# Pooling stage in another order: ACT scales x's columns, the values' products stand behind the pooling products, and the router works on x unscaled

## What is computed

```python
def pool_mixer(h, w, b, scale):          # 4 groups of 256 columns, windows 2, 4, 8, 16
    hg = h.reshape(B, S, N_POOL_GROUPS, POOL_GROUP)
    pooled = stack([centred_mean(hg[:, :, g], POOL_WINDOWS[g]) for g in range(4)])
    y = einsum('bsgc,gcd->bsgd', pooled - hg, w) + b
    return y.reshape(B, S, D_MODEL) * scale

def modulated_sublayer(x, mod, g_pre, g_post, fn, weight):
    shift, scale, gate = mod             # rows of silu(c) @ ada_w + ada_b
    h = rmsnorm(x, g_pre) * (1.0 + scale) + shift
    y = rmsnorm(fn(h), g_post)
    return x + weight * (1.0 + gate) * y

kv = rmsnorm_2(mem, g_mem) @ w_mem_kv    # K and V of the memory tokens, used much later

h2 = rmsnorm_2(x, g_ffn)                 # the router and the experts
g_logits = h2 @ w_rg + b_rg              # 4 groups, the best one is taken
e_logits = h2 @ w_re + b_re              # 32 experts, the best 2 of the group
moe = sum(combine[:, n] * swiglu_n(h2) for n in 32 experts)
```

## Time and profile before

| | |
|---|---|
| median of three | 1756.24 us |
| the profiled execution | 1757.07 us, of which the span 1755.0 |
| PE busy | 1660.3 us (95%) |
| DVE, ACT busy | 1216.7 us (69%), 868.3 us (49%) |
| mean granted clock of PE | 0.967 |
| from K's first product to the first product of the second feed-forward | 239.2 to 319.4 us |
| x behind the mixing to the first expert | 1406.8 to 1438.6 us |

### The profile page before, as it was taken

One profiled execution on the slowest core, in us unless ns is written; L12 is line 12 of the kernel. 1 busy time (PEld: TensorE's weight loads), 2 busy tenths in 40 slices (PEclk: granted clock), 3 DMA queues, 4 the chain that ended last, 5 costly groups with the idle time before them and its releaser, 6 DMA issues.

```text
span 1755.0 us, 19937 instructions
## 1 busy us (share of the span) xinstructions
PE 1660.3 (95%) x7889; PEld 1311.8 (75%) x7889; DVE 1216.7 (69%) x1705; ACT 868.3 (49%) x1239; POOL 51.4 (3%) x81
## 2 busy tenths in 40 slices
PE   6999986999999999989999999999989989999997
PEld 2888864778868888658788878766768787787875
DVE  3989976789856765544655555686577558888986
ACT  3445441534444444346544445544354437777774
POOL 1100000001000000000000001000000010000000
PEclk9999997999999999999999999998599989999999
DMA  9998952988749755340666644452022328989993
GB/s 350 375 348 274 323 169 91 360 304 291 249 148 333 251 190 183 133 144 7 235 215 190 193 138 123 162 163 84 26 107 73 120 73 310 353 315 323 333 332 127
DMA packets 200564, 373.78 MB, mean 213 GB/s; under 512 B 8880, under 2 KB 102486, under 8 KB 200464
## 3 DMA queue, kind: packets, MB, share of 16 engines
q1 hardware_dynamic: 186192, 320.48, 53.8%
q0 software_dynamic: 13872, 50.86, 8.3%
q10 hardware_dynamic: 400, 1.10, 0.2%
HBM read 371.36 MB, written 1.05 MB: 212 GB/s over the span
## 4 chain that ended last, share of the span: by engine, by line
PE 84%; DVE 8%; ACT 5%; DMA 1%; issue 1%; SPq 0%; DVEq 0%; ACTq 0%
PE banks L519 23%; PE banks L521 22%; PE banks L520 22%; PE banks L746 2%; PE banks L1258 1%; PE banks L1285 1%; ACT full L718 1%; DVE ul L463 1%; PE banks L1737 1%; PE banks L872 1%; PE banks L2195 1%; PE banks L671 1%; ACT uh L452 1%; PE banks L2240 1%; PE banks L1272 1%
## 5 line engine op out<-in xcount | busy, mean ns | idle before, releaser
L463 DVE TENSOR_TENSOR ul<-raw,uh 128x1024 fp32r<-128x1024 f32 (+2 forms) x548 | 659.6, 1211 | 253.2 <-ACT uh L452 244.9
L452 ACT ACTIVATE uh<-raw 128x1024 fp32r<-128x1024 f32 (+2 forms) x548 | 571.5, 1050 | 488.1 <-PE banks L521 462.5
L519 PE MATMUL banks<-uh,hh 128*128 128x512 f32 (+2 forms) x1280 | 523.5, 409 | 21.8 <-ACT kvm L1123 15.3
L521 PE MATMUL banks<-uh,hl 128*128 128x512 f32 (+2 forms) x1280 | 501.3, 392 | 0.0
L520 PE MATMUL banks<-ul,hh 128*128 128x512 f32 (+2 forms) x1280 | 500.6, 391 | 0.0
L519 PEld LDWEIGHTS banks<-uh,hh 128*128 128x128 f32 x1280 | 244.5, 191 | 85.4 <-ACT kvm L1123 16.2
L520 PEld LDWEIGHTS banks<-ul,hh 128*128 128x128 f32 x1280 | 244.8, 191 | 53.6 <-issue 7.7
L521 PEld LDWEIGHTS banks<-uh,hl 128*128 128x128 f32 x1280 | 244.1, 191 | 51.0
L519 PE MATMUL banks<-uh,bh 128*128 128x512 f32 x528 | 209.3, 396 | 9.3 <-DVE bl L926 4.2
L521 PE MATMUL banks<-uh,bl 128*128 128x512 f32 x528 | 206.0, 390 | 0.0
L520 PE MATMUL banks<-ul,bh 128*128 128x512 f32 x528 | 205.6, 389 | 0.0
(11 more groups left out here) (310 smaller groups left out, 1412.6 us busy)
## 6 DMA issues: line engine op xcount, KB each, us to landing
raw<-in_ffn_w_in SPq DMA_DIRECT2D x176, 512.0 KB, 5.4
raw<-in_w_up SPq DMA_DIRECT2D x64, 1024.0 KB, 5.8
raw<-in_ffn_w_out SPq DMA_DIRECT2D x44, 1024.0 KB, 7.1
arena<-in_ada_w POOLq DMA_DIRECT2D x42, 1024.0 KB, 8.2
raw<-in_w_down SPq DMA_DIRECT2D x32, 1024.0 KB, 5.6
raw<-in_ada_w SPq DMA_DIRECT2D x30, 1024.0 KB, 6.3
raw<-in_w_in SPq DMA_DIRECT2D x22, 1024.0 KB, 5.1
raw<-in_w_mem_kv SPq DMA_DIRECT2D x4, 1024.0 KB, 6.0
```

What stands on the lines that cost most here:

```text
L452: act.e.activation(uh[r][:, 0:w], raw[m % NRAW][:, h * w:(h + 1) * w], AF.Copy).then_inc(act_done, ta.put("hi", u))
L463: dve.e.tensor_tensor(ul[r][:, 0:w], raw[m % NRAW][:, h * w:(h + 1) * w], uh[r][:, 0:w].bitcast(F32), ALU.subtract).then_inc(dve_done, tv. ...
L519: pe.e.matmul(o, a, wh, start=s0, stop=False)
L521: mm = pe.e.matmul(o, b, wh, start=False, stop=s1)
```

## The change

In the pooling stage:
- `plan`: the pooling weights are loaded ahead of V's, and the gap behind the pooling has no modulation pieces. The two of `ADA_POOL` are now layer 0's pieces 10 and 11 (both gates), and the second feed-forward has ten pieces on DVE instead of eight.
- Splits stop at K's end until K is copied; `kv_act` and `kv_dve` then name by hand which units they split where.
- V's products come in two parts: the first quarter ahead of the pooling products, the rest behind them. V's copies move behind the next norm's root.
- ACT scales x's columns with the shift as bias (from `pool_dve` to `kv_act`). DVE multiplies by counts only at the sequence's ends and has the window's factor in the subtraction; the pooling weights are scaled ahead of it; the bias is held in four rows of 256.
- The second feed-forward's turn uses banks 6, 7, 4, 5 and has no filler ahead of it.

In the router: PE transposes x itself, the gain goes into the router's weights, the row scale into the step that adds the bias. Row 0 and row 1 have logits apart. Filler stands around the counts, `back_pe` behind the first expert's first product, and the router's weights, in another part of the arena, are loaded with the gain.

```diff
+ADA_POOL = [_left.pop(6) for _ in range(2)]
 ADA_AT.update({(0, 0, _b): _left.pop(0) for _b in range(10)})
-ADA_POOL = [_left.pop(0) for _ in range(2)]
-ADA_GAP[0, 0] = [_left.pop(0) for _ in range(2)]
-ADA_AT.update({(0, 1, _b): _left.pop(0) for _b in range(8)})
+ADA_AT.update({(0, 1, _b): _left.pop(0) for _b in range(10)})
...
+    chunks.append((("pw",), [(I["pool_w"][0].rearrange("g (k p) n -> p (g k) n", p=P), 0)], 8, 256, False))
     block(("kv",), I["w_mem_kv_2"][0], 512, 512)
-    chunks.append((("pw",), [(I["pool_w"][0].rearrange("g (k p) n -> p (g k) n", p=P), 0)], 8, 256, False))
-    for a in ADA_GAP[0, 0]:
-        ada(*a)
...
+        kv_units = [u for u, un in enumerate(units) if chunks[un[0]][0] == ("kv",)]
+        k_end, v_end = kv_units[4], kv_units[7] + 1
...
         def kv_pe(pe):
...
             ada_parts_pe(pe, ADA_POOL[1], 7)
-            linear(pe, ("kv",), KD, lh, ll, ready, [[4], [5]], done=("v",))
+            pool_w = take_raw(pe, ("pw",))
+            linear(pe, ("kv",), 2, lh, ll, ready, [[4], [5]], last=False)
+            pool_pe(pe, *pool_w)
+            linear(pe, ("kv",), 6, lambda k, t: lh(k + 2, t), lambda k, t: ll(k + 2, t), lambda k: ready(k + 2),
+                   [[4], [5]], first=False, done=("v",))
...
         def kv_act(act):
...
-            for n, a in enumerate(ADA_POOL):
+            for a in ADA_POOL:
                 ada_skip(act, a)
-                ada_copy_act(act, a, POOL_BANKS[n], START_BUFS[n])
+            skip_raw(act, ("pw",))
+            act.end = k_end + 2
+            split_high(act, act.unit_at + 1)
+            ada_copy_act(act, ADA_POOL[0], POOL_BANKS[0], START_BUFS[0])
+            for g in range(4):
+                act.wait_ge(pe_done, tp("T", 1, g))
+                for k in range(2):
+                    kk = 2 * g + k
+                    act.e.activation(hp[:, kk, 8:264], bank_parts(g)[:, k, :], AF.Identity, bias=ab[:, 1, 1, kk:kk + 1],
+                                     scale=ab[:, 1, 0, kk:kk + 1]).then_inc(act_done, ta.put())
+                ta.same("tf", 1, g)
+            ada_copy_act(act, ADA_POOL[1], POOL_BANKS[1], START_BUFS[1])
+            act.end = v_end + 2
+            split_high(act, act.unit_at + 5)
+            post_act(act, 1, "pool")
+
+        def v_act(act):
             units_act(act, ("kv",), KD)
             act.wait_ge(pe_done, tp("v"))
...
         def kv_dve(dve):
             post_dve(dve, 0, 0.5, "out", 0, NFF - 1)
+            units_dve(dve, ("kv",), KD)
+            for a in ADA_POOL:
+                ada_skip(dve, a)
+            pool_w = take_raw(dve, ("pw",))
+            pool_scale_dve(dve, *pool_w, (0, 1))
+            dve.e.tensor_tensor(pbb[0:4, :], pbb[0:4, :], psr[0:4, :], ALU.mult).then_inc(dve_done, tv.put("pb"))
             diag_dve(dve, 1)
...
+            dve.end = v_end
+            split_low(dve, dve.unit_at)
+            pool_scale_dve(dve, *pool_w, (2, 3))
+            pool_dve(dve)
+            for n, a in enumerate(ADA_POOL):
+                ada_end_dve(dve, a, POOL_BANKS[n])
+            split_low(dve, dve.unit_at + 2)
+            post_dve(dve, 1, 1.0, "pool")
+
+        def v_dve(dve):
             units_dve(dve, ("kv",), KD)
...
         def pool_dve(dve):
...
-                dve.e.tensor_tensor(z, src[:, :, o:o + S], rc[:, g:g + 1, :].to_broadcast([P, 2, S]),
-                                    ALU.mult).then_inc(dve_done, tv.put())
+                for c in (0, S - h) if g else (0,):
+                    e = src[:, :, o + c:o + c + h]
+                    dve.e.tensor_tensor(e, e, rc[:, g:g + 1, c:c + h].to_broadcast([P, 2, h]), ALU.mult).then_inc(
+                        dve_done, tv.put())
                 dve.own()
-                dve.e.tensor_tensor(z, z, hp[:, 2 * g:2 * g + 2, 8:264], ALU.subtract).then_inc(
+                dve.e.scalar_tensor_tensor(zT[:, 2 * g:2 * g + 2, :], src[:, :, o:o + S], 0.5 / h,
+                                           hp[:, 2 * g:2 * g + 2, 8:264], ALU.mult, ALU.subtract).then_inc(
                     dve_done, tv.put("z", g))
...
         def route_pe(pe):
-            keep_busy(pe, 7, 32)
-            pe.wait_ge(dve_done, tv("gx", 1))
+            keep_busy(pe, 7, 10)
...
+                        mm = pe.e.transpose(PB[b][:, k * P:(k + 1) * P], x[:, t, (4 * q + k) * P:(4 * q + k + 1) * P],
+                                            ident[:, :])
...
             gather_pe(pe, 0, 0, 4)
             gather_pe(pe, 0, 1, 5)
-            keep_busy(pe, 6, 18)
-            back_pe(pe, 0)
...
         def route_dve(dve):
...
+            normed(0)
+            for t in range(T):
+                dve.wait_ge(pe_done, tp("logits", t))
+                dve.e.scalar_tensor_tensor(lg[:, t, :], PB[1 + t][:, 0:36], st[:, 6 + t:7 + t], rbias, ALU.mult,
+                                           ALU.add).then_inc(dve_done, tv.put("lg", t))
...
         def experts_pe(pe):
...
                 if b:
                     outp(b - 1)
+                else:
+                    back_pe(pe, 0)
```

More of the change, by code:

```diff
@@ L354, in build @@
         V = A(T, 128)
+        QM_AT = A.at
         QM = A(T, 4, 128)
@@ L1998, in mix_dve @@
             units_dve(dve, ("wo",), KD)
+            dve.wait_ge(loaded("moe"), 16 * 7)
+            g0 = where["g_ffn_2"]
+            dve.e.tensor_tensor(wr, wr, cc[:, g0:g0 + KD].unsqueeze(2).to_broadcast([P, KD, 36]), ALU.mult).then_inc(
+                dve_done, tv.put("wr"))
             dve.wait_ge(pe_done, tp("wo"))
@@ L2044, in route_pe @@
-            pe.wait_ge(loaded("moe"), 16 * 7)
-            pe.take(2)
-            for t in range(T):
+            keep_busy(pe, 7, 10)
+            for t in range(T):
+                pe.wait_ge(dve_done, tv("x", 6, t))
+                for q in range(2):
+                    b = 4 + 2 * t + q
+                    pe.take(b)
+                    for k in range(4):
+                        mm = pe.e.transpose(PB[b][:, k * P:(k + 1) * P], x[:, t, (4 * q + k) * P:(4 * q + k + 1) * P],
+                                            ident[:, :])
+                    mm.then_inc(pe_done, tp.put("T", "hf", t, q))
+                    if (t, q) == (0, 1):
+                        pe.frees(b, act_done, ta, "hf", t, q)
+                    else:
+                        pe.frees(b, dve_done, tv, "hf", t, q)
@@ L2047, in route_pe @@
+            pe.wait_ge(dve_done, tv("wr"))
+            for t in range(T):
+                pe.take(1 + t)
                 for k in range(KD):
[L2048 to L2049 removed]
+                    if (t, k) == (0, 4):
+                        pe.wait_ge(act_done, ta("hf", 0, 1))
                     elif k % 4 == 0:
[L2051 to L2052 removed]
+                        pe.wait_ge(dve_done, tv("hf", t, k // 4))
+                    mm = pe.e.matmul(PB[1 + t][:, 0:36], hf[:, k, t * P:(t + 1) * P], wr[:, k, :],
@@ L2053, in route_pe @@
                                      start=(k == 0), stop=(k == KD - 1))
-            mm.then_inc(pe_done, tp.put("logits"))
-            pe.frees(2, dve_done, tv, "lg")
+                mm.then_inc(pe_done, tp.put("logits", t))
+                pe.frees(1 + t, dve_done, tv, "lg", t)
+            keep_busy(pe, 0, 10)
             pe.take(3)
@@ L2116, in route_dve @@
                 dve_done, tv.put())
+            normed(1)
             c4 = sm_[:, :, 56:60]
```

160 lines of the change are left out of this document (70 added, 90 removed).

## The result

The changed kernel takes 1715.06 us (median of four, 1714.42 to 1716.26; before on the same chip 1756.03), a ratio of 0.9773 with a 95% interval of 0.9753 to 0.9792. The forecast was 1719, its range 1711 to 1734.

| stretch | before | after | difference | forecast |
|---|---|---|---|---|
| start to K's first product | 239.15 | 239.53 | +0.38 | +0.25 |
| K's first product to the pooling's update | 65.71 | 37.77 | -27.94 | -27.55 |
| update to the second feed-forward's first product | 14.51 | 13.81 | -0.70 | -0.05 |
| that feed-forward, to its own update | 197.08 | 195.92 | -1.16 | 0 |
| from there to x's update ahead of the router | 890.36 | 890.33 | -0.03 | 0 |

What follows compares the result with a forecast made beforehand. PE was taken as the bound, on the chain for 84%, held up in the pooling stage and by short dependent router steps. Pooling -27.3 and router -9.9 make -37.2 us: 1757.07 to 1719.9, by the median 1719; range 1711 to 1734.

Steps and rivals of the forecast that it cites:

- steps 1, 2: Pooling stage: PE's pause goes, -15.25 us; V's 13 products behind a busy PE take 2.9 instead of 5.20, -2.3.
- step 3: Pooling stage: three quarters of V's products, 36, go behind the pooling products, -8.1 us.
- step 4: Pooling stage, V's first quarter to the update: 12.7 us instead of 15.36, -2.7, with DVE keeping ahead of PE.
- the 1.7 for the clock: Pooling stage: 1.7 us added for one low-clock stretch, behind the bias run or step 6's wait; 0 and 3.4 kept for range.
- step 6: Update to the feed-forward: 14.05 us instead of 14.51, -0.45, PE waiting some 2 us for V's last low half.
- step 5: First update, ahead of the pooling stage: one split fewer on ACT and one on DVE, -0.9 us.
- the 0.4 for a split between scaled halves: Pooling stage: 0.4 us added because one more split stands between the scaled halves of x that PE waits for.
- no end of the range comes from here: ACT's scaling of x's columns, eight taken as 4.0 us: even at three times the price, z comes before PE's 273.
- zero was forecast: Second feed-forward: two more modulation pieces, +1.7 us on PE, and two totals fewer, -1.7; DVE's sums lie beside PE's products.
- the experts gave nothing back: Rival, experts: weight loads bound them, so the router's lead is waited off later; 1729 us, chance 0.11.
- ACT waited for no load: Rival, pooling stage: ACT becomes the bound, two feed-forward splits ahead of the update's squares wait for a load; +7, 1726, chance 0.07.
- The clock cost one stretch: Rival, pooling stage and router's gather: products behind waits run at the low clock; +6 us, 1725, chance 0.13.

Runs made afterwards that it cites:

- v_end_two: On k_first, splits stop again at V's end until the pooling's sums are done, ACT splitting two units ahead of the update instead of four: 1743.63 us.
- k_first: Kernel before with one thing alone, splits stop at K's end until ACT has copied K: 1756.62 us.
- router_only: Kernel before with the change's router part alone: 1741.47 us.
- v_end: On k_first, splits stop again at V's end until the pooling's sums are done, ACT splitting four units ahead of the update: 1752.15 us.
- pool_only: Kernel before with the change's pooling part alone, router old: 1727.32 us.
- v_ahead: Changed kernel with all four quarters of V's products, and their splits, ahead of the pooling products again: 1727.25 us.
- bias_rows: Changed kernel with the bias's products formed over 128 rows instead of 4: 1714.61 us.
- dve_scale: Changed kernel with x's columns scaled by DVE again instead of ACT: 1722.13 us.
- three: Changed kernel with V's last low half ahead of the update, bias over 128 rows, and the first expert's gated product behind two splits instead of four: 1706.46 us.
- low_early: Changed kernel with DVE's low half of V's last quarter ahead of the update instead of behind it: 1709.28 us.

## Why the prediction was right

The time came 4 us below the forecast, by the forecast's mechanisms. Point by point:

- *The pause and V's clock* (steps 1, 2): both went in full; V's first quarter took 2.94 (2.9). v_end_two and k_first show what the pause stood for: one split in ACT's line held up K's copies and also DVE's sums, and freeing K's copies alone gave nothing.
- *36 products behind the pooling* (step 3) and *the run to the update* (step 4, with the 1.7 for the clock): 14.26 against 14.4. The prediction took one low stretch for two places, without saying which; it came behind the bias (1.86), and not behind the wait of step 6. It also says that PE followed DVE in this stretch before; by the earlier trace rows PE was busy 14.59 of the 15.36 us, and the only wait is the 0.80 ahead of the bias. The sum did not suffer, as it was made of PE's instructions.
- *The first update* (step 5): from K's first product to V's place in PE's line, the pause left out, took 20.57 instead of 21.55, 0.98 less against 0.9.
- *Behind the update* (step 6): PE waited 1.86 for V's last low half, as said; x's turn took 3.62 up to the feed-forward instead of 3.84, and the 0.4 for a split between scaled halves did not show: 0.64 us better than forecast.
- *ACT's scaling*: "no end of the range comes from here" was wrong. I compared its end with the sums alone; PE's bias needs the banks at 263. At DVE's place the same work costs 3.8, so at three times its price, with the last column done at 267.3, it would by the same wait have cost PE some of that too (an estimate; it was not run). ACT's real price, eight in 3.75, kept it harmless.
- *The feed-forward*: zero was forecast, 1.16 came. What the sum left out is a wait: before, PE waited once for DVE's sum of a piece, and that row has no counterpart now:

```profile
353.02 1.12 PE L671 MATMUL banks<-arena,ones 128*128 128x512 f32 x2 [1.23 <-DVE arena L664]
```

  The same wait of 1.23 stands in router_only, k_first, v_end and v_end_two, which have the pieces of the gap, and not in pool_only or v_ahead, which have none. That it is the gap's totals that make DVE late is argued from this, and not shown.

- *The router*: -11.87 against -9.9. The parts, forecast and measured: to the logits 9.3 and 9.08, to the gather 4.9 and 4.51, the gather 4.1 and 3.49, to the gated product 10.45 and 10.03; and the weights' scaling by the gain, put at 0.35, lay wholly beside PE's last products. All five were priced a little high. But 0.97 of it hangs on the clock of one execution: in four of the eight profiles with this router and its filler (router_only, v_ahead, bias_rows, dve_scale) the filler ahead of the counts itself ran partly low, without a pause of PE in front of it, and held up the counts, so that the first gated product came at 28.1 and the router won 10.9. The same row in three and in bias_rows:

```profile
1375.04 2.48 PE L544 MATMUL banks<-sum,ident 128*128 128x128 f32 x20
```

```profile
1384.72 4.10 PE L544 MATMUL banks<-sum,ident 128*128 128x128 f32 x20
```

- *The layers between*: their agreement to 0.03 us is luck. The forecast put no term there, and in the other profiles this part is up to 6.6 us shorter (last section), more than the forecast's whole error.
- *Rivals*: the experts gave nothing back, their 31 steps from the first gated product to the last take 290.63 against 290.98. ACT waited for no load. The clock cost one stretch in the stage and, in the profile of the changed kernel, none in the router. The rule of the Trainium skill that I named for that case ("TensorE: Matmul & The Clock Gate", "HAM oscillation") is borne out in the experiments: behind waits of 9.15, 2.05 and 1.84 us (v_ahead, dve_scale, bias_rows) and around the counts without filler the products ran low. In the changed kernel itself the 12 products behind 1.86 us of waiting ran at 1.00, so the length of a wait alone does not say when.

## What to carry to other kernels

An instruction that waits for a load is dangerous in every in-order line it stands in: look for all of its victims, on that engine and on those that follow it, since freeing one alone moved the wait and gained nothing. When an operation changes engine, ask also who waits for the buffer that it reads. And pulling one step ahead of put-off work pays only if nobody needs that work next.

## What was not expected of the hardware

The mixing of the second block runs partly at the lower clock, and how much differs between kernels that are the same there. These are the stretches 1100 to 1180, within it, of the changed kernel and of low_early:

```profile
1100.00:1180.00 80.00, 76.90 (x317) 57.36 (x317) 62.53 (x115) 37.98 (x51) 0.00 (x0) 0.94 0.45 145
```

```profile
1100.00:1180.00 80.00, 76.91 (x335) 57.32 (x333) 65.05 (x120) 39.01 (x54) 0.00 (x0) 1.00 0.48 158
```

From the second feed-forward's first product to x's update the profiles show 1079.6 (low_early), 1080.7 (v_ahead) and 1081.1 (three), and 1085.0 to 1087.8 in all the others. Counted from that first product, the instruction of ACT that stands at 1036 in the changed kernel comes 1.1 us earlier in low_early, and the one at 1175 comes 7.3 earlier, so most of the difference arises in this mixing. These 4 to 8 us lie outside the stages that the edits change. Why these three fall on the short side was not settled: all three have no wait for V's last low half, but the kernel before has none either (1087.4), and v_ahead's other runs were up to 18 us longer than the profiled one.
